# Expert units of a streaming-encoder kernel loaded as two halves of columns over two queues, with the gate stage and the kernel's beginning reordered

## The chip, the cores and the metric

The kernel runs on one core of one Trainium2 chip. The metric is the device time of one execution in microseconds (us), the median of several runs. All data is float32; the large products of the first half of the kernel are made in split form (a high and a low part of each operand).

## The reference, cut to what matters

One layer of an encoder block on 256 tokens of width 2048. After a normalized input projection, two attention groups and an output projection, the block ends with PEER, a retrieval over 128 x 128 single-neuron experts. The change lies in PEER and in the first microseconds of the input projection:

```python
h = rmsnorm(x, g_attn)
proj = h @ w_in                                   # the kernel's first stage
...
x = x + concat(y_a, y_b) @ w_o
hb = rmsnorm(x, g_ffn)
qr = (hb @ w_pq).reshape(b, t, 8, 2, 128)
sc = einsum('bthpd,hpnd->bthpn', qr, sub_keys)
s_top, i_top = top_k(sc, 16)                      # per half of the key
c_top, c_pos = top_k(s_top[..., 0, :, None] + s_top[..., 1, None, :], 16)
expert = i0 * 128 + i1
g = softmax(c_top)
a = gelu(einsum('bthkd,btd->bthk', u_tab[expert], hb))
x = x + einsum('bthk,bthkd->btd', g * a, v_tab[expert])
```

Each of the tables u_tab and v_tab has 16384 rows of 2048 floats, 134 MB.

## The kernel before, in words

The program is written per engine, with semaphores between the engines; the order on each engine is written out by hand.

**The first half** multiplies token tiles with pieces of w_in, w_o and w_pq. SyncE loads a piece of 512 KB (`load`, L355) into one of four buffers `raw`, ScalarE makes its high part (`split_hi`, L538), VectorE the low part (`split_lo`, L809), and TensorE makes twelve products per piece (`tall_unit`, L1307). At the very beginning the transposed tokens `xT` come in eight parts, each ahead of its piece of w_in on SyncE's queue; ScalarE and VectorE scale and split them (`norm_hi`, `norm_lo`). GpSimd's queue issues six small constants first (L437 to L442), then the rows of x and other weights, paced by `piece_used`, the count of half pieces that TensorE has finished.

**PEER** treats the 256 tokens in two ways. For 96 tokens (three of each four of the first 128, `N_SP`) the picked rows are fetched: GpSimd gathers one row of u_tab per partition and step, 1 MB in all, into one of five row buffers (`gather`, L471), and VectorE multiplies and sums it (`next_row`, L1128). A gather waits until the row five before it was used. There are 96 such rows of u_tab (`N_OWN`) and then 96 of v_tab; the latter are also paced by TensorE's count of finished units, from unit 117 to unit 250 (`PACE_FROM`, `PACE_TO`). For the other 160 tokens (`N_DN`) TensorE multiplies with the whole tables: 128 units of u_tab (`u_chunk`, L1511), then 128 of v_tab (`v_chunk`, L1567). A unit is 128 experts x 2048, 1 MB, 8 KB in each of 128 partitions, and is used in 16 products, each of two matmul instructions. Four ring buffers hold units; the transfer into a buffer is issued when the unit four before it is used up (`unit_used`): even units by SyncE (L404, L409), odd ones by ScalarE behind its gelu (`odd_unit`, L769). TensorE waits once per unit for its semaphore `unit_in`.

**The gates.** While TensorE works on the first 48 units of u_tab, VectorE finds the picks (`top_k`) and uses 28 rows. At unit 44 ScalarE takes the exponentials; VectorE then makes the gates' table of slots, uses rows in between, and from unit 48 (`FIRST_G`) on builds for each group of four tokens two one-hot tables (`hots`, L1179), which ScalarE scales by the gates (`hot_scale`, L755, eight and four operations, behind the gelu of a fixed unit, `scale_after`). TensorE multiplies them (`gate_group`, L1530), and VectorE applies them to finished activations (`gate`, L1190) and to each new unit's (`apply`, L1201). Gelu results of these units go through two buffers, so that ScalarE waits for the `apply` of two units before. TensorE does groups 0 and 1 behind units 50 and 51, and the others each behind an even unit; there are 40.

VectorE's program from unit 52 on is a loop in which rows stand between the gates' steps:

```python
for c in range(FIRST_G + 4, NKEY):
    ... hots(g + 1) if c is even, else gate(g)
    apply(c - 1)
    if rows_done[0] < N_OWN and c % 8 != 7:
        next_row()
    if c == WEIGH_AT: ...
```

Of the kernel before, what the change touches and what calls it, by code (L numbers as in the profile page):

```python
# [18 lines left out]
def build_block(nc, io):  # L19
# [5 lines left out]
    ACT = mybir.ActivationFunctionType  # L25
    AX = mybir.AxisListType.X
    ds = bass.ds
# [50 lines left out]
    with ExitStack() as ctx:  # L78
# [164 lines left out]
        unit_in = [sem(f"unit_in{i}") for i in range(NRING)]  # L243
# [4 lines left out]
        lent_in, acc_sum = sem("lent_in"), sem("acc_sum")  # L248
# [83 lines left out]
        WEIGH_AT = NKEY - 8  # L332
# [21 lines left out]
        def _(sp):  # L354
# [9 lines left out]
            for n in range(8):  # L364
                k = slice(2 * n, 2 * n + 2)
                sp.dma_start(xT[:, k, :], io["xT"][:, k, :]).then_inc(xT_in[n], 16)
                if n == 0:
                    sp.dma_start(gains[:, :], io["gains"]).then_inc(gain_in, 16)
                load(n, n, win[:, k, 0:512])
# [24 lines left out]

            for j in range(2):
                sp.wait_ge(lo_done, 2 * (B_U + 2 * j + 1) - 2 * (NRAW - 1))
                sp.dma_start(ring[j], u_unit(j)).then_inc(unit_in[j], 16)
            sp.wait_ge(piece_used, 2 * B_U)
            for j in range(2, NRING):
                sp.dma_start(ring[j], u_unit(j)).then_inc(unit_in[j], 16)  # L400
            with sp.Fori(1, NKEY // NRING) as i:
                for j in range(0, NRING, 2):
                    sp.wait_ge(unit_used, i * NRING + (j + 1 - NRING))
                    sp.dma_start(ring[j], u_unit(i * NRING + j)).then_inc(unit_in[j], 16)  # L404

            def v_units(i):
                for j in range(0, NRING, 2):
                    sp.wait_ge(unit_used, i * NRING + (NKEY + j + 1 - NRING))
                    sp.dma_start(ring[j], io["v_tab"][ds(i * (NRING * P) + j * P, P), :]).then_inc(unit_in[j], 16)  # L409
# [25 lines left out]
        def _(pool):  # L435

            pool.dma_start(acts[0:32, A_BIAS:A_BIAS + 512], io["bucket_hot"]).then_inc(hot_in, 16)  # L437
            pool.dma_start(acts[0:32, A_BIAS + 512:A_BIAS + 520], io["rel_bias"]).then_inc(hot_in, 16)
            pool.dma_start(iota[:, :], io["iota"]).then_inc(mask_in, 16)
# [88 lines left out]
        def _(act):  # L528
# [85 lines left out]

            act.wait_ge(gain_in, 16)
# [153 lines left out]
            def odd_unit(c):  # L769

                act.wait_ge(unit_used, c + 1 - NRING)
                src = io["u_tab"] if c < NKEY else io["v_tab"]
                act.dma_start(ring[c % NRING], src[c % NKEY * P:c % NKEY * P + P, :]).then_inc(unit_in[c % NRING], 16)

            for c in range(NKEY):
                gelu(c)
                if c % 2:
                    odd_unit(c + NRING)
                if c == FIRST_G - 4:
                    act.wait_ge(slot_ready, TT * NH)  # L780
                    nc.scalar.activation(slot[:, 2, :], slot[:, 2, :], ACT.Exp).then_inc(cexp_done, 1)
                if c in scale_after:
                    hot_scale(scale_after[c])
                if c == WEIGH_AT - 2:
                    act.wait_ge(row_used, N_OWN)
                    nc.scalar.activation(a_sel, a_sel, ACT.Gelu).then_inc(a_done, 1)
            for c in range(NKEY + 1, 2 * NKEY - NRING, 2):
                odd_unit(c + NRING)
# [9 lines left out]
        def _(dve):  # L798
# [35 lines left out]
            link(V.memset(kpad, 0.0))  # L834
# [383 lines left out]
            next_row(4)  # L1218
# [11 lines left out]
            next_row(2)  # L1230
            apply(FIRST_G)
            next_row()
# [8 lines left out]
            for c in range(FIRST_G + 4, NKEY):  # L1241
                if c % 2 == 0:
                    if g + 1 < N_GRP:
                        hots(g + 1)
                else:
                    gate(g)
                    g += 1
                apply(c - 1)
                if rows_done[0] < N_OWN and c % 8 != 7:
                    next_row()  # L1250
                if c == WEIGH_AT:
                    assert rows_done[0] == N_OWN
                    dve.wait_ge(a_done, 1)
                    dve.wait_ge(gsp_in, 48)
                    V.tensor_tensor(w_sp[:, 0:N_OWN], a_sel, w_sp[:, 0:N_OWN], ALU.mult).then_inc(w_ready, 1)
                    dve.wait_ge(acc_in, 16)
                    dve.wait_ge(mask_set, 2)
                    V.tensor_scalar(acc, acc, own_row, None, ALU.mult).then_inc(acc_set, 1)
                    dve.wait_ge(w_ready, 1)
                    dve.wait_ge(acc_set, 1)  # L1260
                if c > WEIGH_AT and c % 2:
                    next_row()
# [27 lines left out]
        def _(pe):  # L1290
# [99 lines left out]

            for j in range(8):
# [119 lines left out]
            def u_chunk(i, q):  # L1511
# [5 lines left out]
                pe.wait_ge(unit_in[q], i * 16 + 16)  # L1517
                for k in range(KD):
                    ins = mm(ps[:, q, 0:N_DN], ring[q][:, k * P:k * P + P], hF[:, k, :], start=k == 0, stop=k == KD - 1)  # L1519
# [47 lines left out]
            def v_chunk(i, q, first=False, last=False):  # L1567

                pe.wait_ge(unit_in[q], i * 16 + (16 * NKEY // NRING + 16))
                for k in range(KD):  # L1570
                    if first and k == 8:
                        pe.wait_ge(gelu_done, NKEY)
# [82 lines left out]
```

## Time and profile before

| | us |
|---|---|
| median of 3 runs | 1678.68 (1678.19 to 1679.05) |
| the profiled execution's own time | 1682.57 |
| its span, first to last instruction | 1680.8 |
| TensorE busy | 1653.3 |
| VectorE busy | 1019.2 |
| ScalarE busy | 503.3 |
| GpSimd busy | 293.3 |
| moved by DMA | 569.90 MB, 339 GB/s over the span |

Busy TensorE time is modelled for pipelined matmuls, so a short wait shows best as a gap named in a timeline. The span divides into: input and output projections and attention (to about 400 us), the query projection (to about 508), units of u_tab (514 to 1116, the gates from about 727 on) and units of v_tab (1116 to 1671).

### The profile page before, as it was taken

How to read it: one execution, taken by the hardware profiler on the slowest of the kernel's cores; microseconds unless marked ns; L12 is line 12 of the kernel's file. 1: busy time of each engine (PE TensorE's matmuls, PEld its weight loads, DVE VectorE, ACT ScalarE, POOL GpSimd, SP SyncE). 2: the span in 40 equal slices, each digit the busy share in tenths (PEclk: the TensorE clock that was granted, in tenths of full speed). 3: DMA queues.
4: the chain of work that ended last, by engine and by line, in shares of the span. 5: the costliest groups of instructions: out<-in, count | busy, mean ns of one | idle time of the engine just before them, and what ended most of it. 6: DMA issues, size and time to landing. Idle time of an engine off the chain costs nothing.

```text
span 1680.8 us, 28829 instructions
## 1 busy us (share of the span) xinstructions
PE 1653.3 (98%) x11428; PEld 1568.1 (93%) x11428; DVE 1019.2 (61%) x1708; ACT 503.3 (30%) x1346; POOL 293.3 (17%) x252
## 2 busy tenths in 40 slices
PE   7999999999999999989999999999999999999999
PEld 5768888888999999979999999999999999999998
DVE  5426695767778999767777667663334333433343
ACT  6547567656551000134454444420000000000000
POOL 1020000000003222322212111122212212223220
PEclk9999999999999999999999999999999999999999
DMA  9764445466648999999999999999999999999996
GB/s 337 240 142 131 138 132 194 138 223 204 224 154 347 421 403 421 397 400 421 394 422 406 421 408 422 375 388 416 417 415 417 417 416 422 422 422 422 421 417 236
DMA packets 107056, 569.90 MB, mean 339 GB/s; under 512 B 11280, under 2 KB 13456, under 8 KB 48208
## 3 DMA queue, kind: packets, MB, share of 16 engines
q1 hardware_dynamic: 57056, 216.51, 34.8%
q0 software_dynamic: 31792, 220.50, 32.7%
q10 hardware_dynamic: 18144, 132.13, 19.2%
q8 instruction: 29, 0.48, 0.1%
q14 instruction: 35, 0.29, 0.0%
HBM read 563.04 MB, written 4.46 MB: 338 GB/s over the span
## 4 chain that ended last, share of the span: by engine, by line
PE 78%; DVE 12%; DMA 6%; ACT 1%; issue 1%; POOL 1%; SPq 0%; DVEq 0%; ACTq 0%; POOLq 0%
PE ps L1574 32%; PE ps L1519 19%; PE ps L1315 5%; PE ps L1317 5%; PE ps L1316 5%; DVE late L1136 3%; PE ps L1334 2%; PE ps L1468 2%; PE ps L1536 2%; PE ps L1470 2%; PE ps L1469 2%; DMA raw<-in_w_in 1%; DMA acts<-in_u_rows,sel 1%; DMA late<-in_u_rows,sel 1%; DVE w_lo L817 1%
## 5 line engine op out<-in xcount | busy, mean ns | idle before, releaser
L1140 DVE SCALAR_TENSOR_TENSOR acts<-late,sel,acts 128x2048 f32<-128x2048 f32 x77 | 181.1, 2351 | 246.5 <-DMA late<-in_v_tab,sel 246.1
L1519 PE MATMUL ps<-acts,raw 128*128 128x160 f32 x2048 | 289.3, 301 | 0.0
L1519 PE MATMUL ps<-acts,late 128*128 128x160 f32 x2048 | 287.9, 300 | 0.0
L1574 PE MATMUL ps<-acts,late 128*128 (+1 forms) x2048 | 284.2, 299 | 0.0
L1574 PE MATMUL ps<-acts,raw 128*128 (+1 forms) x2048 | 283.6, 300 | 0.2 <-DMA raw<-in_v_tab 0.2
L1519 PEld LDWEIGHTS ps<-acts,raw 128*128 128x128 f32 x2048 | 282.1, 191 | 0.0
L1519 PEld LDWEIGHTS ps<-acts,late 128*128 128x128 f32 x2048 | 280.5, 190 | 0.0
L1574 PEld LDWEIGHTS ps<-acts,raw 128*128 128x128 f32 x2048 | 279.9, 190 | 0.6 <-issue 0.6
L1574 PEld LDWEIGHTS ps<-acts,late 128*128 128x128 f32 x2048 | 280.1, 190 | 0.1
L817 DVE TENSOR_TENSOR w_lo<-raw,w_hi 128x512 fp32r<-128x512 f32 (+1 forms) x288 | 188.8, 682 | 134.9 <-ACT w_hi L544 132.9
L1315 PE MATMUL ps<-w_hi,hT_hi 128*128 128x512 f32 (+1 forms) x448 | 185.7, 415 | 13.5 <-DVE w_lo L817 13.2
L544 ACT ACTIVATE w_hi<-raw 128x512 fp32r<-128x512 f32 (+1 forms) x288 | 170.2, 622 | 90.2 <-PE ps L1470 42.3
L1136 DVE SCALAR_TENSOR_TENSOR late<-late,acts 128x2048 f32<-128x2048 f32 x76 | 173.1, 2287 | 14.3 <-DMA late<-in_u_rows,sel 14.1
L1317 PE MATMUL ps<-w_hi,hT_lo 128*128 128x512 f32 (+1 forms) x448 | 174.4, 389 | 0.0
L1316 PE MATMUL ps<-w_lo,hT_hi 128*128 128x512 f32 (+1 forms) x448 | 173.8, 388 | 0.0
L483 POOL DMA_INDIRECT late<-in_v_tab,sel x77 | 106.9, 1389 | 370.7 <-PE ps L1574 261.5
L793 ACT ACTIVATE acts<-ps 128x320 f32<-128x320 f32 x8 | 3.5, 437 | 555.9 <-PE ps L1574 555.7
L483 POOL DMA_INDIRECT late<-in_u_rows,sel x76 | 95.8, 1261 | 302.8 <-DVE late L1136 236.6
L1315 PEld LDWEIGHTS ps<-w_hi,hT_hi 128*128 128x128 f32 x448 | 84.7, 189 | 36.3 <-issue 14.8
L1316 PEld LDWEIGHTS ps<-w_lo,hT_hi 128*128 128x128 f32 x448 | 84.8, 189 | 17.5 <-issue 3.1
L1317 PEld LDWEIGHTS ps<-w_hi,hT_lo 128*128 128x128 f32 x448 | 84.4, 188 | 17.2
L1198 DVE TENSOR_TENSOR acts<-acts,ps 128x512 f32<-128x512 f32 x40 | 46.6, 1166 | 84.6 <-PE ps L1536 84.6
(220 smaller groups left out, 1575.7 us busy)
## 6 DMA issues: line engine op xcount, KB each, us to landing
raw<-in_w_in SPq DMA_DIRECT2D x72, 512.0 KB, 3.7
raw<-in_u_tab SPq DMA_DIRECT2D x33, 1024.0 KB, 9.7
late<-in_u_tab SPq DMA_DIRECT2D x33, 1024.0 KB, 9.9
raw<-in_v_tab SPq DMA_DIRECT2D x32, 1024.0 KB, 9.3
raw<-in_v_tab ACTq DMA_DIRECT2D x32, 1024.0 KB, 9.2
late<-in_v_tab SPq DMA_DIRECT2D x32, 1024.0 KB, 9.1
late<-in_v_tab ACTq DMA_DIRECT2D x32, 1024.0 KB, 9.3
raw<-in_u_tab ACTq DMA_DIRECT2D x31, 1024.0 KB, 9.7
```

The lines of the kernel that those rows point to most:

```text
L483: pool.indirect_dma_start(row[n % NROW], None, table, bass.IndirectOffsetOnAxis(ap=idx[:, k:k + 1], axis=0)).then_inc(row_in[n % NROW], 16)
L544: nc.scalar.activation(whi[(2 * j + half) % NPART][:, 0:w], raw[j % NRAW][:, half * w:half * w + w], ACT.Copy).then_inc(hi_done, 1)
L817: V.tensor_tensor(wlo[slot_no][:, 0:w], raw[j % NRAW][:, half * w:half * w + w], whi[slot_no][:, 0:w].bitcast(F32), ALU.subtract).then_inc ...
L1136: V.scalar_tensor_tensor(row[n % NROW], row[n % NROW], 1.0, hs[turn % 2], ALU.mult, ALU.mult, accum_out=a_sel[:, n:n + 1]).then_inc(row_us ...
L1140: V.scalar_tensor_tensor(acc, row[n % NROW], w_sp[:, n - N_OWN:n - N_OWN + 1], acc, ALU.mult, ALU.add).then_inc(row_used, 1)
L1198: V.tensor_tensor(a, a, ps[:, 4 + g % 2, :].rearrange("p (t e) -> p t e", t=4), ALU.mult).then_inc(gated, 1)
L1315: mm(out, hT_hi[:, k, t], whi[part][:, 0:w], start=start and kk == 0, stop=False)
L1316: mm(out, hT_hi[:, k, t], wlo[part][:, 0:w], start=False, stop=False)
L1317: ins = mm(out, hT_lo[:, k, t], whi[part][:, 0:w], start=False, stop=stop and kk == 1)
L1334: ins = mm(ps[:, bank, :], src[:, k, b * P:b * P + P], w[:, k, :], start=k == 0, stop=k == ks - 1)
L1519: ins = mm(ps[:, q, 0:N_DN], ring[q][:, k * P:k * P + P], hF[:, k, :], start=k == 0, stop=k == KD - 1)
L1574: ins = mm(ps[:, pair_bank(k // 2), at:at + N_DN], ring[q][:, k * P:k * P + P], acts[:, ds(i * (4 * N_DN) + q * N_DN, N_DN)], start=first ...
```

## The change

1. A unit is loaded in two halves of 1024 columns (4 KB in each partition): SyncE issues the first half of every unit, ScalarE the second half of every unit from the fifth on (`second_half`); both halves of the first four units are issued by SyncE. Each half has its own semaphore, and TensorE waits for the second one ahead of the ninth of its 16 products.
2. Behind the slots' table VectorE uses 2 rows rather than 4, none behind the first hot tables (2 before), and none between the first two `apply` (1 before). In the loop it leaves out a row at every sixteenth unit rather than at every eighth, and the weighing step of the gathered rows stands at unit 122 rather than 120.
3. At the beginning `xT`'s first part and `gains` are issued by ScalarE, so w_in's first piece is SyncE's first transfer; four of the six constants on GpSimd's queue wait until TensorE has finished a half piece; ScalarE runs a one-element operation, with the load of its function table, ahead of its first wait for data; TensorE makes five products of zeros ahead of its first wait.

```diff
-        unit_in = [sem(f"unit_in{i}") for i in range(NRING)]
+        unit_in = [sem(f"unit_in{i}") for i in range(2 * NRING)]
...
-        WEIGH_AT = NKEY - 8
+        WEIGH_AT = NKEY - 6
...
             for n in range(8):
                 k = slice(2 * n, 2 * n + 2)
-                sp.dma_start(xT[:, k, :], io["xT"][:, k, :]).then_inc(xT_in[n], 16)
-                if n == 0:
-                    sp.dma_start(gains[:, :], io["gains"]).then_inc(gain_in, 16)
+                if n:
+                    sp.dma_start(xT[:, k, :], io["xT"][:, k, :]).then_inc(xT_in[n], 16)
                 load(n, n, win[:, k, 0:512])
...
             with sp.Fori(1, NKEY // NRING) as i:
-                for j in range(0, NRING, 2):
+                for j in range(NRING):
                     sp.wait_ge(unit_used, i * NRING + (j + 1 - NRING))
-                    sp.dma_start(ring[j], u_unit(i * NRING + j)).then_inc(unit_in[j], 16)
+                    sp.dma_start(ring[j][:, 0:HALF], u_unit(i * NRING + j)[:, 0:HALF]).then_inc(unit_in[2 * j], 16)
...
+            pool.wait_ge(piece_used, 1)
             pool.dma_start(iota[:, :], io["iota"]).then_inc(mask_in, 16)
...
+            act.dma_start(xT[:, 0:2, :], io["xT"][:, 0:2, :]).then_inc(xT_in[0], 16)
+            act.dma_start(gains[:, :], io["gains"]).then_inc(gain_in, 16)
+            act.wait_ge(warm_set, 1)
+            nc.scalar.activation(table_warm, carrier, ACT.Copy)
...
-            def odd_unit(c):
+            def second_half(c):
 
                 act.wait_ge(unit_used, c + 1 - NRING)
                 src = io["u_tab"] if c < NKEY else io["v_tab"]
-                act.dma_start(ring[c % NRING], src[c % NKEY * P:c % NKEY * P + P, :]).then_inc(unit_in[c % NRING], 16)
+                act.dma_start(ring[c % NRING][:, D // 2:D], src[c % NKEY * P:c % NKEY * P + P, D // 2:D]).then_inc(unit_in[2 * (c % NRING) + 1], 16)
 
             for c in range(NKEY):
                 gelu(c)
-                if c % 2:
-                    odd_unit(c + NRING)
+                second_half(c + NRING)
...
-            link(V.memset(kpad, 0.0))
+            V.memset(carrier, 0.0).then_inc(warm_set, 1)
+            V.memset(kpad, 0.0).then_inc(warm_set, 1)
...
-            next_row(4)
+            next_row(2)
...
             hots(0)
             hots(1)
-            next_row(2)
             apply(FIRST_G)
-            next_row()
             apply(FIRST_G + 1)
             next_row()
             gate(0)
...
-                if rows_done[0] < N_OWN and c % 8 != 7:
+                if rows_done[0] < N_OWN and c % 16 != 15:
                     next_row()
...
+            pe.wait_ge(warm_set, 2)
+            for _ in range(5):
+                mm(ps[:, 6, 0:256], kpad[:, 0, :], early[:, 1024:1280], start=True, stop=True)
...
-                pe.wait_ge(unit_in[q], i * 16 + 16)
                 for k in range(KD):
+                    if k % 8 == 0:
+                        pe.wait_ge(unit_in[2 * q + k // 8], i * 16 + 16)
                     ins = mm(ps[:, q, 0:N_DN], ring[q][:, k * P:k * P + P], hF[:, k, :], start=k == 0, stop=k == KD - 1)
```

**VectorE, from the hot tables of groups 0 and 1 on, before.** L1184 builds one-hot tables, L1136 uses a gathered row, L1208 is `apply`, L1198 is `gate`.

```order
L1184 TENSOR_TENSOR early<-iota,slotT 128x512 x2
L1184 TENSOR_TENSOR acts<-iota,slotT 128x512 x2
L1136 SCALAR_TENSOR_TENSOR late,sel<-late,acts 128x2048 x2
L1208 TENSOR_TENSOR acts<-acts,early 128x160
L1136 SCALAR_TENSOR_TENSOR late,sel<-late,acts 128x2048
L1208 TENSOR_TENSOR acts<-acts,early 128x160
L1136 SCALAR_TENSOR_TENSOR acts,sel<-acts 128x2048
L1198 TENSOR_TENSOR acts<-acts,ps 128x4x128
L1184 TENSOR_TENSOR early<-iota,slotT 128x512 x2
```

The same place now; the lines have moved on by seven.

```order
L1191 TENSOR_TENSOR early<-iota,slotT 128x512 x2
L1191 TENSOR_TENSOR acts<-iota,slotT 128x512 x2
L1215 TENSOR_TENSOR acts<-acts,early 128x160 x2
L1143 SCALAR_TENSOR_TENSOR acts,sel<-acts 128x2048
L1205 TENSOR_TENSOR acts<-acts,ps 128x4x128
L1191 TENSOR_TENSOR early<-iota,slotT 128x512 x2
```

Between the tables of group 1 and those of group 2 stood four rows; one is left, behind both `apply`.

**ScalarE, at the first units of u_tab, before.** L753 is the gelu of a unit, L773 the issue of an odd unit's transfer.

```order
L753 ACTIVATE acts<-ps 128x160 [waits x2_stored]
L753 ACTIVATE acts<-ps 128x160 [waits unit_used]
L773 DMA raw<-in_u_tab 128x2048 [waits unit_used]
L753 ACTIVATE acts<-ps 128x160 [waits unit_used] x2
L773 DMA late<-in_u_tab 128x2048 [waits unit_used]
```

The same place now:

```order
L760 ACTIVATE acts<-ps 128x160 [waits x2_stored]
L780 DMA raw<-in_u_tab 128x1024 [waits unit_used]
L760 ACTIVATE acts<-ps 128x160 [waits unit_used]
L780 DMA raw<-in_u_tab 128x1024 [waits unit_used]
L760 ACTIVATE acts<-ps 128x160 [waits unit_used]
L780 DMA late<-in_u_tab 128x1024 [waits unit_used]
```

There is an issue of half the size behind every gelu, where there was one of the full size behind every second; SyncE's loop likewise has one of half the size per unit.

## Rows read from the trace of the kernel before

**Rows 1.** Busy time by stage: PE, PEld, DVE, ACT, POOL, clock, DMA share, GB/s

```profile
530.00:600.00 70.00, 70.00 (x517) 69.97 (x516) 63.38 (x196) 4.86 (x16) 18.43 (x11) 1.00 1.01 422
...
850.00:1055.00 205.00, 204.83 (x1645) 201.88 (x1645) 146.98 (x183) 95.20 (x308) 39.12 (x39) 1.00 1.01 416
...
1400.00:1600.00 200.00, 200.00 (x1474) 200.00 (x1473) 82.47 (x36) 0.00 (x0) 49.84 (x35) 1.00 1.01 422
```

**Rows 2.** The chain that ended last, in v_tab's stage: start, us, what

```profile
1364.06 13.10 DMA raw<-in_v_tab
1377.29 293.12 PE ps L1574 x2156
```

**Rows 3.** Timeline of PE at the wait for that unit

```profile
1377.29 8.01 PE L1574 MATMUL ps<-acts,raw 128*128 x57 [0.22 <-DMA raw<-in_v_tab]
```

**Rows 4.** DMA issues of the page: KB each, median us to landing

```profile
late<-in_u_tab SPq DMA_DIRECT2D x33, 1024.0 KB, 9.9
```

**Rows 5.** Timeline of PE where the gates begin

```profile
746.09 0.84 PE L1536 MATMUL ps<-acts 128*128 128x128 bf16 x12 [2.88 <-ACT acts L766]
...
757.18 1.46 PE L1536 MATMUL ps<-early 128*128 128x128 bf16 x12 [5.85 <-ACT early L766]
```

**Rows 6.** Busy time in the stretch of that second wait, columns as in rows 1

```profile
754.00:762.00 8.00, 4.82 (x26) 4.82 (x27) 7.90 (x11) 3.28 (x12) 4.12 (x6) 0.57 1.01 422
```

**Rows 7.** Timeline of DVE where the gates begin

```profile
728.97 1.29 DVE L1184 TENSOR_TENSOR acts<-iota,slotT 128x512 bf16<-128x512 f32 x2
...
734.18 2.29 DVE L1136 SCALAR_TENSOR_TENSOR late<-late,acts 128x2048 f32<-128x2048 f32 x1 [3.92 <-DMA late<-in_u_rows,sel]
...
741.67 0.32 DVE L1208 TENSOR_TENSOR acts<-acts,early 128x160 f32<-128x160 f32 x1
...
748.77 2.29 DVE L1136 SCALAR_TENSOR_TENSOR acts<-acts 128x2048 f32<-128x2048 f32 x1 [1.20 <-DMA acts<-in_u_rows,sel]
...
750.99 1.16 DVE L1198 TENSOR_TENSOR acts<-acts,ps 128x512 f32<-128x512 f32 x1
...
752.06 1.28 DVE L1184 TENSOR_TENSOR early<-iota,slotT 128x512 bf16<-128x512 f32 x2
```

**Rows 8.** Timeline of ACT where the gates begin

```profile
733.76 0.30 ACT L753 ACTIVATE early<-ps 128x160 f32<-128x160 f32 x1 [4.04 <-PE ps L1519]
...
742.09 0.30 ACT L753 ACTIVATE early<-ps 128x160 f32<-128x160 f32 x1 [4.18 <-DVE acts L1208]
...
753.38 2.44 ACT L762 ACTIVATE early<-early,acts 128x128 bf16<-128x128 bf16 x8 [5.41 <-DVE early L1184]
755.85 1.28 ACT L766 ACTIVATE early<-early,slotT 128x128 bf16<-128x128 bf16 x4
...
774.15 0.30 ACT L753 ACTIVATE early<-ps 128x160 f32<-128x160 f32 x1 [4.83 <-PE ps L1519]
```

**Rows 9.** Timeline of ACT in the steady gate stage, gelu of two odd units

```profile
1058.94 0.30 ACT L753 ACTIVATE early<-ps 128x160 f32<-128x160 f32 x1 [4.83 <-PE ps L1519]
...
1068.42 0.30 ACT L753 ACTIVATE early<-ps 128x160 f32<-128x160 f32 x1 [4.83 <-PE ps L1519]
```

**Rows 10.** Timeline of POOL: gathers of rows 32 and 37

```profile
722.14 2.40 POOL L483 DMA_INDIRECT late<-in_u_rows,sel  x1 [16.70 <-DMA sel<-sel]
...
736.75 0.94 POOL L483 DMA_INDIRECT late<-in_u_rows,sel  x1 [6.88 <-DVE late L1136]
```

**Rows 11.** SyncE's DMA queue, 1400 to 1600 us: packets, MB, share of 16 engines

```profile
q1 hardware_dynamic: 3327, 24.12, 29.0%
```

**Rows 12.** The same queue with pieces of w_pq, 422 to 426 us

```profile
q1 hardware_dynamic: 389, 1.40, 85.7%
```

**Rows 13.** The same queue with pieces of w_pq, 412 to 500 us

```profile
q1 hardware_dynamic: 4043, 14.70, 50.4%
```

**Rows 14.** ACT's first table load, and DMA in the chain's beginning

```profile
3.57 1.28 ACT L564 ACT_TABLE_LOAD   x1 [3.57 <-DMA acts<-in_xT]
...
17.73 12.63 DMA raw<-in_w_in
```

More of the change, by code:

```diff
@@ L247, in build_block @@
         hs_in, idx_in, gsp_in, mask_set, acc_set, turn_kept = sem("hs_in"), sem("idx_in"), sem("gsp_in"), sem("mask_set"), sem("acc_set"), sem("turn_kept")
-        lent_in, acc_sum = sem("lent_in"), sem("acc_sum")
+        lent_in, acc_sum, warm_set = sem("lent_in"), sem("acc_sum"), sem("warm_set")
         gsp_ready, a_done, w_ready, acc_in = sem("gsp_ready"), sem("a_done"), sem("w_ready"), sem("acc_in")
@@ L393, in u_unit @@
                 return io["u_tab"][ds(v * P, P), :]
+            HALF = D // 2
             for j in range(2):
                 sp.wait_ge(lo_done, 2 * (B_U + 2 * j + 1) - 2 * (NRAW - 1))
-                sp.dma_start(ring[j], u_unit(j)).then_inc(unit_in[j], 16)
+                for h in range(2):
+                    sp.dma_start(ring[j][:, HALF * h:HALF * h + HALF], u_unit(j)[:, HALF * h:HALF * h + HALF]).then_inc(unit_in[2 * j + h], 16)
             sp.wait_ge(piece_used, 2 * B_U)
             for j in range(2, NRING):
-                sp.dma_start(ring[j], u_unit(j)).then_inc(unit_in[j], 16)
+                for h in range(2):
+                    sp.dma_start(ring[j][:, HALF * h:HALF * h + HALF], u_unit(j)[:, HALF * h:HALF * h + HALF]).then_inc(unit_in[2 * j + h], 16)
             with sp.Fori(1, NKEY // NRING) as i:
-                for j in range(0, NRING, 2):
+                for j in range(NRING):
                     sp.wait_ge(unit_used, i * NRING + (j + 1 - NRING))
-                    sp.dma_start(ring[j], u_unit(i * NRING + j)).then_inc(unit_in[j], 16)
+                    sp.dma_start(ring[j][:, 0:HALF], u_unit(i * NRING + j)[:, 0:HALF]).then_inc(unit_in[2 * j], 16)
             def v_units(i):
-                for j in range(0, NRING, 2):
+                for j in range(NRING):
                     sp.wait_ge(unit_used, i * NRING + (NKEY + j + 1 - NRING))
-                    sp.dma_start(ring[j], io["v_tab"][ds(i * (NRING * P) + j * P, P), :]).then_inc(unit_in[j], 16)
+                    sp.dma_start(ring[j][:, 0:HALF], io["v_tab"][ds(i * (NRING * P) + j * P, P), 0:HALF]).then_inc(unit_in[2 * j], 16)
             with sp.Fori(0, 8) as i:
@@ L786, in _ @@
                     nc.scalar.activation(a_sel, a_sel, ACT.Gelu).then_inc(a_done, 1)
-            for c in range(NKEY + 1, 2 * NKEY - NRING, 2):
-                odd_unit(c + NRING)
+            for c in range(NKEY, 2 * NKEY - NRING):
+                second_half(c + NRING)
             for p in range(KD // 2):
@@ L1567, in v_chunk @@
             def v_chunk(i, q, first=False, last=False):
-                pe.wait_ge(unit_in[q], i * 16 + (16 * NKEY // NRING + 16))
                 for k in range(KD):
+                    if k % 8 == 0:
+                        pe.wait_ge(unit_in[2 * q + k // 8], i * 16 + (16 * NKEY // NRING + 16))
                     if first and k == 8:
```

## The prediction, made before the changed kernel ran

> **What bounds the kernel now.** I read the stage table first. From 530 us on TensorE is busy for the whole of each stretch, and the 16 DMA engines are too, at 416 to 422 GB/s [rows 1]. VectorE and ScalarE have room: 147 and 95 of 205 us in the gate stage. So two limits lie on top of each other, and a step counts only as far as it moves the one that ends last.
>
> TensorE's own pace is 293.12 us for 2156 matmuls, 0.136 us each, so 4.35 us for a unit of 32 [rows 2]. A gate group adds the rest of a pair: two gelus of odd units lie 9.48 us apart [rows 9], which less two units leaves 0.78 us.
>
> The transfers' pace: 1.049 MB at 422 GB/s is 2.485 us for a unit or a gathered row. In the gate stage 7 rows go with 8 units, so a unit's share is 2.485 x 1.875 = 4.66 us, against 9.48/2 = 4.74 us of TensorE. In v_tab's stage 96 rows are paced over 133 units, 0.722 each: 4.28 against 4.35 us. Both leave only some 1.7%. A unit's transfer may take three units of TensorE, 13.05 us; the median takes 9.9 [rows 4], and one of v_tab took 13.10 [rows 2] and made TensorE wait 0.22 us [rows 3].
>
> TensorE's one large loss is where the gates begin: it waits 2.88 and 5.85 us for ScalarE's scaled tables [rows 5]. In the stretch of the second wait the granted clock is 0.57 on average, so partly the 1.2 GHz level, and the group behind it takes 1.46 us instead of 0.84 [rows 5, 6]. All in all: between the gelus of units 49 and 55 lie 774.15 - 733.76 = 40.39 us [rows 8], and the work is 6 x 4.35 + 4 x 0.78 = 29.2. **11.2 us are lost.**
>
> **Part 1, the rows taken out of the gates' beginning.** VectorE finishes the tables of groups 0 and 1 at 730.26, and then stands in front of rows still in transfer, four waits from 3.92 to 1.20 us [rows 7]. So the first `apply` comes at 741.67 although its gelu was done, ScalarE's gelu of unit 50 waits for it until 742.09, and the table of group 2 is begun at 752.06, for which ScalarE waits 5.41 us [rows 7, 8]. In the new order both `apply` follow the tables at once (unit 49's at 734.1, behind its gelu), and the single row left, number 30, was gathered long before: 2.3 us, to 736.7. I step on with the same durations. ScalarE scales group 0 from 734.2 for 2.45 + 1.28 us, to 737.9; TensorE ends unit 50 at 738.1 and does the group, to 738.9; VectorE gates it to 740.1 (1.16) and builds group 2's table to 741.4 (1.28). ScalarE scales group 1 from 738.9 to 742.7, ahead of unit 51's end at 743.2, and group 2 from 743.7 to 747.5, ahead of unit 52's end at 748.3. No wait is left, and with it goes the low clock. **-11.2 us**; the bound from the other side is that the larger wait stays.
>
> Rows held back: gathers 35 and 36 start only when rows 30 and 31 are used (about 737 and 744), where before five were issued from 722.14 on [rows 10]. They are wanted at about 760 and 765, so nothing waits for them. Five rows must be made up in the loop: 64 rows from unit 52 on at 15 in 16 units end at unit 119, as the 59 before did, ahead of the weighing at 122. VectorE gains one row of 2.29 us per 16 units, 0.14 us a unit, covered by its idle quarter [rows 1]. The price is in the transfers: 0.0625 x 2.485 = 0.155 us a unit.
>
> **Part 2, the halves.** The additional issues lie beside free time of SyncE and behind ScalarE's gelu, where an issue stood already behind every second one. TensorE's additional wait, when already met, costs nothing: 2156 matmuls with 67 met waits keep one pitch of 0.136 us [rows 2]. Bytes stay equal, but packets are 4 KB rather than 8. SyncE's queue moved 24.12 MB in 29.0% of 3200 engine-us, 26.0 GB/s per engine [rows 11]. With w_pq's packets of 4 KB and little beside it, 1.40 MB took 85.7% of 64, 25.5 GB/s [rows 12], 2% less. The far end is all of w_pq's stage, 14.70 MB in 50.4% of 1408, 20.7 GB/s [rows 13], a quarter less, but there the engines mostly idled between pieces; the near end is nothing. I take 2%, so 2.535 us a unit.
>
> With both, a unit of the gate stage asks for 2.535 + 0.9375 x 2.485 = 4.865 us of transfer against 4.74 of TensorE. Over the 68 units from 52 to 119 the arrears are 8.5 us. They are first paid from the time that a transfer may take. Both halves of a unit now run side by side, behind the previous unit's only; sharing the engines with a row, a unit needs about 2 x 2.535 us and some 2 us to be reported (an estimate, from the 9.9 us of a unit that shared with two others [rows 4]), so 7 to 8 us of 13.05. That pays about 6; **+2.4 us** wait remains (0 to 8.5). In v_tab's stage the demand is 2.535 + 1.794 = 4.33 against 4.35, with x2's reload of 1.3 MB on top, which before was enough for the 13.10: **+1.0** (0 to 4). At u_tab's beginning, where five rows and four units are in flight at once at 422 GB/s [rows 1], I put **+1.0** (0 to 2).
>
> The Trainium skill ("DMA: Bandwidth & Descriptors", section Bandwidth) speaks against the halves: it asks for transfers of at least 1 MiB for 75% of peak. By that rule the 512 KB halves would lose far more than 2%; the traced queue at 85.7% with 512 KB pieces doesn't bear it out.
>
> **Part 3, the beginning.** ScalarE's table load of 1.28 us [rows 14] goes beside the wait for data, w_in's first piece is issued two issues sooner, and four constants leave its way. But up to about 30 us transfers end last: the piece issued at 17.73 takes 12.63 us [rows 14], and the bytes until then are the same, since the constants only move behind the first half piece. TensorE's five products at the start warm a stretch that waits for data anyway. I take **-1.0** (0 to -2.5).
>
> **The sum**: -11.2 - 1.0 + 2.4 + 1.0 + 1.0 = -7.8 us. Against the profiled execution's 1682.57 that is 1674.8. The median of the runs lies 3.9 us lower, at 1678.68, and I put the same difference there: **1670.9 us**.
>
> **The rivals.**
> - *Transfers cover themselves.* Without the three added waits: -12.2, **1666.5**. For it: units waited only 0.22 us at 98% load [rows 3], and waiting by halves gives the second half 2.2 us more. Chance 0.20.
> - *The wait moves.* Rows 34 to 36 come later than I step them, or one scaled table is late, and a wait of the size of the larger one (5.85) stays with its low clock: -7.8 + 5.9 = -1.9, **1676.8**. ScalarE supports it: in the steady stage it ends a table just as its group is due. Chance 0.15.
> - *The transfers bound the gate stage: slower.* If a half costs 3.5% more, a unit takes 2.57 us; two queues of 4 KB packets against one of 8 KB rows hold only half of the engines, which is less than the units' share, so units are late rather than rows, and nothing is paid from the slack. Then each unit asks 4.90 against 4.74, 68 x 0.16 = 11; v_tab's 4.366 against 4.35, 2; the reload 3; the beginning of u_tab 1.5. -12.2 + 17.5 = +5.3, **1684.0**. It turns slower once less than about a third of the arrears can be paid from slack. Against it: 422 GB/s held for 200 us with all queues active [rows 1]. Chance 0.13.
> - *Halves flow like all of w_pq's stage*, 26% longer, 3.12 us: 0.71 x 68 + 0.56 x 128 + 0.2 x 48 = 130 us more, about **1797**. The skill's rule points this way. Chance 0.02.
>
> **How the numbers follow.** My forecast has 0.50. Its own range is 1668 to 1675. With the first rival at the low end, and the second and a part of the third at the high one: 1665.5 to 1681. A measurement tells 0.2%, 3.4 us. Faster by more: the forecast, the first rival and a third of the second, 0.74; within: the rest of the second and mild forms of the third, 0.13; slower 0.13.
>
> **What would show it.** Right: VectorE's tables of group 2 are built near 741, TensorE's waits of 2.88 and 5.85 are gone and the clock there is 1.00; TensorE shows a few waits named for transfers of u_tab between units 90 and 120, 2 to 3 us together; the share of DMA stays at 1.0 through the gate stage at 410 to 420 GB/s; halves land in 7 to 10 us. Wrong: DMA waits above 8 us in the gate stage, GB/s below 405 at full share, a wait over 3 us near 745 to 760, or a beginning that differs by more than 2.5 us at 60 us.

## The result, and the profile after

The changed kernel takes **1690.41 us** (median of 4 runs, 1688.94 to 1691.05), the kernel before 1678.87 (4 runs, 1678.19 to 1680.11): a ratio of 1.0063, 95% interval 1.0051 to 1.0075. That is **slower** by 11.5 us, where 7.8 us less were forecast, and it lies above the range (to 1681.0). The profiled execution of the changed kernel took 1690.0 us, with a span of 1688.2.

Its busy time by stage, with the columns of [rows 1]:

```profile
530.00:600.00 70.00, 64.90 (x453) 63.11 (x452) 66.69 (x200) 4.25 (x14) 18.95 (x11) 0.98 1.02 411
534.00:574.00 40.00, 37.68 (x256) 36.35 (x256) 38.48 (x118) 2.34 (x8) 9.99 (x6) 0.96 1.02 414
...
850.00:1055.00 205.00, 203.40 (x1631) 200.12 (x1629) 147.37 (x182) 91.13 (x295) 42.16 (x40) 1.00 1.02 415
1400.00:1500.00 100.00, 99.56 (x732) 99.21 (x732) 40.87 (x19) 0.00 (x0) 15.88 (x16) 1.00 1.02 414
```

The engines' share of DMA is full as before, but they move 411 to 415 GB/s rather than 416 to 422, and TensorE is no longer always busy. What it waited for (us in total, times, longest), from the changed kernel's list of waits for the whole execution:

```profile
...
PE ps L1584 <- DMA raw<-in_v_tab: 5.2, 7, 2.5
PE ps L1528 <- DMA raw<-in_u_tab: 3.8, 4, 2.6
PE ps L1584 <- DMA late<-in_v_tab: 2.1, 5, 0.5
...
PE ps L1545 <- ACT early L773: 0.9, 2, 0.5
PE ps L1545 <- ACT acts L773: 0.5, 1, 0.5
PE ps L1528 <- DMA late<-in_u_tab: 0.5, 2, 0.3
...
```

The two waits of [rows 5], 8.7 us for ScalarE's scaled tables, have shrunk to 1.4 us. In their place stand 11.6 us of waits for units of u_tab and v_tab, where before there were 0.22 [rows 3]. The timeline of TensorE at u_tab's beginning:

```profile
533.75 10.63 PE L1528 MATMUL ps<-acts,raw 128*128 128x160 f32 x64 [2.60 <-DMA raw<-in_u_tab]
544.22 4.51 PE L1528 MATMUL ps<-acts,late 128*128 128x160 f32 x32
548.98 4.58 PE L1528 MATMUL ps<-acts,late 128*128 128x160 f32 x32 [0.26 <-DMA late<-in_u_tab]
553.94 4.61 PE L1528 MATMUL ps<-acts,raw 128*128 128x160 f32 x32 [0.37 <-DMA raw<-in_u_tab]
559.04 4.58 PE L1528 MATMUL ps<-acts,raw 128*128 128x160 f32 x32 [0.49 <-DMA raw<-in_u_tab]
```

The first 64 matmuls behind the wait of 2.60 take 10.63 us rather than 8.86, and the granted clock over 534 to 574 us is 0.96: the wait costs more than its length. Later units begin 4.96, 5.10 us and so on apart, rather than 4.35. The shown gaps are only 0.3 to 0.5 us because the matmuls before them are drawn longer, so I count by the starts of units.

The table below gives the start of a unit's first product on TensorE, minus the start of the same unit in the trace of before. "Halves alone" and "order alone" are two experiments told of below (`e2_halves_only` and `e8_order_only`).

| unit | before, us | changed | halves alone | order alone |
|---|---|---|---|---|
| 0 (u_tab) | 515.51 | -2.45 | -2.12 | -0.95 |
| 16 | 585.12 | +6.79 | +6.89 | -1.00 |
| 48 | 724.87 | +6.79 | +6.89 | -1.01 |
| 54 (gates begun) | 764.47 | -4.49 | -4.38 | -12.28 |
| 80 | 887.76 | -4.49 | -4.40 | -12.30 |
| 128 (v_tab) | 1115.91 | -2.10 | -3.40 | -12.55 |
| 160 | 1255.00 | +0.68 | -3.40 | -12.55 |
| 200 | 1429.55 | +7.38 | +2.67 | -11.42 |
| 255 | 1668.61 | +7.38 | +2.82 | -11.42 |

The changed kernel loses 9.2 us over units 0 to 16, gains 11.3 where the gates begin, loses 2.4 in the gate stage and 9.5 in v_tab's. The gain is the forecast one; the losses are not. The first row also shows by how much one execution differs from another: "halves alone" and "order alone" have the old beginning and still start 2.1 and 1.0 us sooner. The trace of before is itself of an execution of 1682.57 us, 3.7 above its kernel's median, and that of the changed kernel of one of 1690.0. So the table ends at +7.4, while the medians lie 11.5 apart: it shows where time goes, and not the size of the whole to a microsecond or two.

Where the gates begin, TensorE's timeline now has no wait, and the granted clock of 748 to 756 us is 1.00, against 0.57 over 754 to 762 us in [rows 6]:

```profile
744.75 0.84 PE L1545 MATMUL ps<-early 128*128 128x128 bf16 x12
745.43 4.57 PE L1528 MATMUL ps<-acts,late 128*128 128x160 f32 x32
749.83 0.83 PE L1545 MATMUL ps<-acts 128*128 128x128 bf16 x12
750.50 4.57 PE L1528 MATMUL ps<-acts,raw 128*128 128x160 f32 x32
754.91 0.83 PE L1545 MATMUL ps<-early 128*128 128x128 bf16 x12
```

What each DMA queue moved between 548 and 558 us (packets, MB, share of 16 engines; q0 carries GpSimd's rows, q1 SyncE's transfers, q10 ScalarE's), in the kernel before:

```profile
q0 software_dynamic: 251, 1.81, 43.5%
q10 hardware_dynamic: 182, 1.36, 32.7%
q1 hardware_dynamic: 144, 1.05, 25.2%
```

The same window of the changed kernel:

```profile
q0 software_dynamic: 283, 2.06, 50.0%
q1 hardware_dynamic: 283, 1.03, 25.7%
q10 hardware_dynamic: 284, 1.03, 25.5%
```

Three queues with work, 283, 283 and 284 packets. But a packet of a row is 8 KB and one of a half is 4 KB, so the rows get half of all bytes, and both halves together the other half. A unit then lands only as often as a row does: 2.10 MB for both at 414 GB/s are 5.07 us, which is TensorE's new pace. The chain that ended last shows how long the halves that TensorE waited for were in flight (start, us, what), where a whole unit's median was 9.9 [rows 4]:

```profile
517.75 15.96 DMA raw<-in_u_tab
...
540.22 13.68 DMA raw<-in_u_tab
...
558.74 15.35 DMA raw<-in_u_tab
...
1131.63 15.15 DMA late<-in_v_tab
...
1260.22 15.34 DMA raw<-in_v_tab
```

That is more than the 13.05 us that a transfer may take.

### The profile page after: what moved, and what is told of

Its sections match the earlier page's. It is cut to its first block, busy times and chain, and to the rows that moved or that the text cites. A ratio compares the mean times of both kernels' runs of the same rounds, so it can differ in the third digit from the quotient of the medians.

```text
span 1688.2 us, 29406 instructions
## 1 busy us (share of the span) xinstructions
PE 1661.3 (98%) x11438; PEld 1571.4 (93%) x11438; DVE 1019.6 (60%) x1709; ACT 503.5 (30%) x1347; POOL 272.5 (16%) x252
## 4 chain that ended last, share of the span: by engine, by line
PE 82%; DMA 12%; DVE 2%; ACT 2%; issue 1%; POOL 0%; ACTq 0%; SPq 0%; DVEq 0%
PE ps L1584 28%; PE ps L1528 26%; PE ps L1320 5%; PE ps L1322 5%; PE ps L1321 5%; DMA raw<-in_v_tab 3%; DMA raw<-in_u_tab 3%; DMA late<-in_v_tab 3%; PE ps L1339 2%; PE ps L1476 2%; PE ps L1478 2%; PE ps L1477 2%; PE ps L1545 1%; DMA sel<-sel 1%; DMA late<-in_u_rows,sel 1%
## 5 line engine op out<-in xcount | busy, mean ns | idle before, releaser
L486 POOL DMA_INDIRECT late<-in_v_tab,sel x77 | 89.1, 1157 | 386.4 <-PE ps L1584 230.8
L760 ACT ACTIVATE early<-ps 128x160 f32<-128x160 f32 x80 | 24.3, 303 | 201.8 <-PE ps L1528 177.4
```

Of the source, the lines that this page charges most:

```text
L486: pool.indirect_dma_start(row[n % NROW], None, table, bass.IndirectOffsetOnAxis(ap=idx[:, k:k + 1], axis=0)).then_inc(row_in[n % NROW], 16)
```

## The experiments

The theories. **A, turns:** the engines take packets from the queues with work in turn; halving a unit's packets halves the weight of its queue against the rows. **B, price of small packets:** bytes in 4 KB packets flow more slowly. **C, order:** the new order of rows makes a backlog that the units run into. **D, the join:** a unit needs two transfers over two queues, and the later one sets it. Where a median is given for before, it is that of runs on the same chip beside the experiment. Most of the expected totals were missed by some microseconds; the stages say more than they.

### Order and beginning without the halves; halves without them

`e1_order_start` is the changed kernel with whole units, as before:

```diff
-                for j in range(NRING):
+                for j in range(0, NRING, 2):
                     sp.wait_ge(unit_used, i * NRING + (j + 1 - NRING))
-                    sp.dma_start(ring[j][:, 0:HALF], u_unit(i * NRING + j)[:, 0:HALF]).then_inc(unit_in[2 * j], 16)
+                    sp.dma_start(ring[j], u_unit(i * NRING + j)).then_inc(unit_in[j], 16)
```

> The changed kernel with whole units again (one transfer of 1 MB and 8 KB packets per unit, even units by SyncE, odd ones by ScalarE); the new order of the gates and the new beginning stay. Theory A (the halves lose: the DMA engines take packets from their queues in turn, so two queues of 4 KB packets hold as much as one queue of 8 KB row packets, and a unit lands every 5.05 us while rows are in backlog): the 2.45 us of the beginning and the 11.3 us of the gates' beginning are gained, the waits for units at the start of u_tab (9.2 us) and in v_tab (9.5 us) are gone; 1665 to 1667 us. Theory B (4 KB packets only move fewer bytes, 414 against 422 GB/s): the same, 1665 to 1668. Theory C (the new order of the rows makes the backlog): waits for units stay in v_tab or move into the gate stage, 1673 or more.

Measured: 1671.15 us against 1680.07, ratio 0.9943 (0.9927 to 0.9960). TensorE waits for no unit of u_tab, so the halves are what makes them late. The total lies above the 1665 to 1668 of theories A and B and below C's 1673: in the gate stage 4.2 us are lost between units 91 and 114, where scaled tables are late.

`e2_halves_only` is the kernel before with the halves, and nothing else of the change.

> The kernel before with nothing but the halves of columns over two queues. Theories A and B: the waits for units of 9.2 us at the start of u_tab and of about 9.5 us in v_tab come, the gates' first wait of 11.2 us stays; 1695 to 1700 us. Theory C (order): the halves alone cost at most the 2% of packet size, under 4 us; 1679 to 1683.

Measured: 1686.61 against 1680.07, ratio 1.0044 (1.0028 to 1.0061). The halves alone make it slower, with the old order: C is not needed. The 1695 to 1700 us of theories A and B were missed all the same, and the table above shows why. This kernel has the old order of rows, and yet it gains 11.3 us between units 48 and 54, as much as the reordered ones. TensorE's timeline there:

```profile
744.86 0.84 PE L1539 MATMUL ps<-early 128*128 128x128 bf16 x12
745.54 4.57 PE L1522 MATMUL ps<-acts,late 128*128 128x160 f32 x32
749.94 0.83 PE L1539 MATMUL ps<-acts 128*128 128x128 bf16 x12
750.61 4.57 PE L1522 MATMUL ps<-acts,raw 128*128 128x160 f32 x32
755.01 0.83 PE L1539 MATMUL ps<-early 128*128 128x128 bf16 x12
```

VectorE's timeline tells why. The tables of group 1, and the first row behind them, which in [rows 7] came at 734.18 after a wait of 3.92 us:

```profile
735.76 1.29 DVE L1186 TENSOR_TENSOR acts<-iota,slotT 128x512 bf16<-128x512 f32 x2
736.97 2.28 DVE L1138 SCALAR_TENSOR_TENSOR late<-late,acts 128x2048 f32<-128x2048 f32 x1
```

The tables are 6.8 us later than in [rows 7], because TensorE, and with it the slots' transposition, is 6.9 us later. The gather of the row behind them did not move back with it. In GpSimd's timeline it is issued at 713.90, where it was 722.14 [rows 10]:

```profile
713.90 0.96 POOL L486 DMA_INDIRECT late<-in_u_rows,sel  x1 [13.04 <-DMA sel<-sel]
```

So between this row's gather and the end of the tables lie 23.1 us, where it was 8.1, and it has landed. The four behind it were issued by 731.77 (728.57 before) and are used from 739.17 on. The time lost on units at u_tab's beginning was given back here, if not by itself alone: how much the sooner gather does and how much the later tables was not tried apart.

### Where one part of the change is undone or done alone

`e8_order_only` is the kernel before with part 2's order of rows, `e9_start_only` the kernel before with the new beginning.

> The kernel before with nothing but the new order of rows and gates. The gates' beginning gains 11.2 us, the gate stage gives about 4.3 back, no start gain: 1672 to 1675 us. If the gain of the beginning (2.5 to 3.6 us in the traces) is real and independent, this run lies that much above the run with whole units, new order and new beginning.

Measured: 1670.97 against 1679.5, ratio 0.9947 (0.9928 to 0.9966), -8.5 us. That is under the 1672 to 1675 expected. Its gain lies between units 48 and 54 (-11.3 by the table); it loses nothing in the gate stage and 1.1 us in v_tab's. There is no wait for units of u_tab.

> The kernel before with nothing but the new beginning (ScalarE issues xT's first part and gains, four constants later, table load and five products ahead of the data). In the traces unit 0 of u_tab starts 2.5 to 3.6 us sooner with the new beginning, but in two runs with the old one it started 1.0 and 2.1 us sooner too. Theory G (a gain of its own of 1 to 2 us, the rest is difference between executions): 1677.0 to 1678.5 beside about 1679.5. Forecast as on record: -1.0. Theory H (full 2.5 to 3.6): 1676 or less.

Measured: 1678.77 against 1679.16, ratio 0.9995 (0.9987 to 1.0004): no gain that can be told. The old order's wait stands here, but once, with 6.45 us. Between units 48 and 54 this trace (of an execution of 1678.69 us) loses 2.1 us less than that of before (1682.57), so the old order costs 9.2 us there in one execution and 11.3 in the other.

Alone, the parts come to -8.5 (order), +6.5 (halves) and -0.4 (beginning), -2.4 in all; together they are +11.5. Of the 14 us between, 9.2 to 11.3 are the same gain counted twice: halves or order, either removes the wait. The rest is of the size of what differs from unit 80 on: 11.9 us are lost in the changed kernel, 7.2 with the halves alone. Of these 4.7 us, 2.8 come over units 128 to 136, at v_tab's beginning, where the changed kernel waits for four units and the other for none.

### How the halves are cut, and the queues

`e3_part_halves` cuts a unit by partitions, 0 to 63 and 64 to 127, so that packets stay at 8 KB; TensorE waits for both ahead of its first product:

```diff
-                    sp.dma_start(ring[j][:, 0:HALF], u_unit(i * NRING + j)[:, 0:HALF]).then_inc(unit_in[2 * j], 16)
+                    sp.dma_start(ring[j][0:64, :], io["u_tab"][ds(i * (NRING * P) + j * P, 64), :]).then_inc(unit_in[2 * j], 16)
```

> The changed kernel with halves of partitions instead of columns: each half 64 partitions of 8 KB, first half by SyncE, second by ScalarE, both awaited ahead of the unit's first product. Packets are 8 KB again. Theory A (packets in turn): the units' two queues hold two thirds of the engines in a backlog, no wait for units; 1665 to 1668. Theory B (bytes per packet): also 1665 to 1668, 422 GB/s. Theory D (two queues, the join of two transfers or the issue of a half behind ScalarE's gelu makes units late, whatever the packets): waits stay, 1686 or more.

Measured: 2298.93 against 1680.07, ratio 1.371 (1.3654 to 1.3766), a miss of every theory. Its busy time by stage:

```profile
530.00:600.00 70.00, 50.90 (x346) 48.72 (x347) 40.98 (x121) 3.04 (x10) 5.62 (x6) 0.95 1.02 261
...
850.00:1055.00 205.00, 142.12 (x1019) 138.30 (x1019) 90.47 (x111) 60.31 (x195) 26.66 (x28) 0.85 1.00 254
```

The engines are busy all the time and move 254 to 261 GB/s; the rows, which are unchanged, slow down with the units (0.94 MB between 548 and 558 us, where the changed kernel moved 2.06). So this run says nothing on A or D, and the same packets had to be cut in another way.

`e5_even_odd` takes even partitions by SyncE and odd ones by ScalarE:

```diff
-                    sp.dma_start(ring[j][:, 0:HALF], u_unit(i * NRING + j)[:, 0:HALF]).then_inc(unit_in[2 * j], 16)
+                    sp.dma_start(ring[j][0:P:2, :], by_two("u_tab")[0, ds(i * (NRING * 64) + j * 64, 64), :]).then_inc(unit_in[2 * j], 16)
```

> The changed kernel with halves of alternate partitions: SyncE loads the 64 even ones, ScalarE the 64 odd ones, 8 KB packets, both awaited ahead of the first product. It asks the question of the run with partitions 0 to 63 and 64 to 127 again, without filling one half of the partitions at a time. Theory A (packets in turn): units hold two thirds of the engines in a backlog, the waits for units at the start of u_tab (9.2 us in the changed kernel) and in v_tab (9.5) go, 1668 to 1673 us as with whole units. Theory D (two queues or the join make units late): the waits stay, 1686 or more. Theory E (any transfer to 64 partitions is slow): far slower, over 1750.

Measured: 1675.23 (10 runs) against 1679.5, ratio 0.9973 (0.9964 to 0.9983). Halves, two queues, a wait for both, the new order: all is there, and it is faster than before. Only the packet has its 8 KB again. Its queues between 548 and 558 us:

```profile
q0 software_dynamic: 237, 1.74, 41.9%
q10 hardware_dynamic: 186, 1.25, 30.1%
q1 hardware_dynamic: 185, 1.24, 29.8%
```

The units have about 60% of the bytes. The time lies 2 us above A's range and 11 below D's. Each measured against its own runs of before, it is 4 to 5 us slower than whole units (`e1_order_start`). By its unit starts it loses 1.1 us over units 0 to 16, where `e1_order_start` loses nothing, and 5.0 us in the gate stage (units 54 to 128), where that one loses 4.2. This bounds what D can be.

`e4_one_queue` is the changed kernel with both column halves issued by SyncE.

> The changed kernel with both halves of columns issued by SyncE, one behind the other, and none by ScalarE: packets of 4 KB, in one queue. Theory A: in a backlog one 4 KB packet of a unit goes with each 8 KB packet of rows, so a unit lands only every 2.57 + 2 x 2.49 = 7.5 us while rows are in backlog; TensorE waits over 3 us per unit there, more than 20 us on top of the changed kernel: 1710 us or more, and the row queue moves about 1.8 to 2 times the bytes of the unit queue in the first 50 us of u_tab. Theory B: as the changed kernel, 1688 to 1692. Theory D: faster than the changed kernel, since no half is issued behind the gelu.

Measured: 1697.0 (one run) against 1680.07. The units have one turn in two rather than two in three. Between 528 and 538 us:

```profile
q0 software_dynamic: 381, 2.74, 66.0%
q1 hardware_dynamic: 381, 1.43, 35.4%
```

Equal packets again, and twice the bytes for the rows. But theory A's total, 1710 us or more, was missed by 13 us: by the starts of units this kernel loses 9.5 us over units 0 to 16, hardly more than the changed kernel's 9.2, and 11.2 in the gate stage rather than 2.4. Between 548 and 558 us q1 already has 56.2%. That the backlog of at most five rows is used up by then fits this, but wasn't tried apart.

`e6_rows_4k` is the changed kernel with each row gathered in two transfers of 4 KB packets, so that all packets are equal:

```diff
-                pool.indirect_dma_start(row[n % NROW], None, table, bass.IndirectOffsetOnAxis(ap=idx[:, k:k + 1], axis=0)).then_inc(row_in[n % NROW], 16)
+                for h in range(2):
+                    pool.indirect_dma_start(row[n % NROW][:, D // 2 * h:D // 2 * h + D // 2], None, table, bass.IndirectOffsetOnAxis(ap=idx[:, k:k + 1], axis=0), element_offset=D // 2 * h).then_inc(row_in[n % NROW], 16)
```

> The changed kernel with each gathered row fetched as two gathers of 1024 columns, so that all three queues have 4 KB packets. Theory A: in the first 50 us of u_tab the three queues move equal packets and so a third of the bytes each, units two thirds; TensorE's waits for units there fall from 9.2 us to under 2, and rows come later (VectorE waits more). Theory B (fewer bytes per packet of 4 KB): waits for units grow, since now all packets are small. Total 1680 to 1695, rows then being what is late in the gate stage.

Measured: 1701.62 (one run) against 1679.5, above the 1680 to 1695 expected. Between 548 and 558 us the rows' queue moved 1.63 MB, the others 1.25 and 1.22. TensorE waits for no unit at all in the whole execution; its waits are these:

```profile
PE ps L1546 <- ACT early L774: 10.1, 3, 7.0
PE ps L1546 <- ACT acts L774: 9.1, 2, 8.0
PE ps L1321 <- DVE w_lo L824: 6.0, 7, 2.8
```

It reaches unit 54 at -14.41 by the table's count, as the order forecasts, and then the rows are late, VectorE's tables behind them, and TensorE waits through ScalarE. Another 10.2 us are lost behind unit 254, where the last rows of v_tab come late too (VectorE uses the last one from 1684.14 us on). So smaller packets for the rows only move the wait. This is the sharpest test of A: still smaller packets, and the waits for units vanish. It also sizes B, by its busy time by stage:

```profile
530.00:600.00 70.00, 70.00 (x517) 70.00 (x517) 62.54 (x197) 5.17 (x17) 30.05 (x22) 1.00 1.03 409
...
1400.00:1600.00 200.00, 200.00 (x1475) 200.00 (x1474) 76.75 (x35) 0.00 (x0) 62.05 (x65) 1.00 1.03 410
```

With every packet of rows and units at 4 KB the engines move 409 and 410 GB/s in these two stretches, with a mix 411 and 414, with 8 KB 422.

`e11_three_rows` is the changed kernel with at most three rows in flight for the first 20 rows rather than five.

```diff
-                if n >= NROW:
-                    pool.wait_ge(row_used, n + 1 - NROW)
+                if n >= NROW or n >= 3:
+                    pool.wait_ge(row_used, n + 1 - (3 if n < 20 else NROW))
```

> The changed kernel with at most three gathers in flight instead of five for rows 0 to 19, the start of u_tab. Theory A (units wait only while rows stand in backlog beside them, since packets go in turn): a shorter backlog, so the waits there fall from 9.2 us to under 5. Theory B (fewer bytes per packet): bytes and packets are equal, 8 to 10 us stay. The rest as in the changed kernel; 1683 to 1688 with A.

Measured: 1690.87 (one run) against 1679.16, above the 1683 to 1688 of theory A. By the starts, unit 16 stands at +1.68 after -2.94 for unit 0: 4.6 us lost there rather than 9.2, as a shorter backlog should make it. Another 4.2 us are lost over units 32 to 48, where five may be in flight again; so that unit 54 stands at -5.44, against -4.49. In v_tab's stage it loses some 11 us, the changed kernel 9.5, and nothing is left of the gain at the end.

### Versions that beat both

`e7_rows_spread` is `e1_order_start` with two rows used ahead of the wait for the exponentials, a row left out at every ninth unit, and the weighing step at unit 124:

```diff
+            next_row(2)
             dve.wait_ge(cexp_done, 1)
...
-                if rows_done[0] < N_OWN and c % 16 != 15:
+                if rows_done[0] < N_OWN and c % 9 != 8:
```

> Whole units, the new beginning, the new gates' order, but rows asked for more evenly: two rows are used ahead of the wait for the exponentials (where VectorE idles 9.4 us), and 62 rows rather than 64 are spread over 70 units rather than 68 (weighing at unit 124). Theory F (in the run with whole units the 4.3 us lost between units 80 and 112 come from the rows' demand of 15 in 16 units, 4.82 us of transfer per 4.74 us unit): those 4.3 us fall below 1.5, 1666 to 1669 us. If they came from something else in the new order: 1670 to 1673.

Measured: 1669.41 against 1679.5 (1666 to 1669 were expected), ratio 0.9938 (0.9919 to 0.9957). Units 54 to 128 keep their lead (-13.81 to -14.39), where `e1_order_start` fell from -14.90 to -10.67.

`e10_reload_spread` is that kernel with SyncE's eight transfers of x2's reload spread over 16 groups of units rather than eight, since 1.4 us were lost there.

> The run with whole units, new beginning, new gates' order and rows spread over 70 units, and x2's reload of 1.3 MB in addition spread over 64 units of v_tab rather than 32. The 1.4 us that TensorE lost there between units 160 and 192 come from the reload on top of 98% load: they go, 1.4 us less than that run's 1669.4, so 1667.5 to 1668.5. If it is only the paced rows that made the unit late: no difference.

Measured: **1668.16** (5 runs, 1667.63 to 1669.49) against 1679.16, ratio 0.9932 (0.9919 to 0.9945), the fastest of all. By its starts v_tab's stage loses 0.4 us rather than 1.4. That it beats the one before it by 1.2 us is at the edge of what can be told across chips.

## Why the prediction was wrong, step by step

**The limits** were read rightly: TensorE and the DMA engines on top of each other with 1.7% between them. The conclusion was drawn only for the sum of bytes, not for who gets them.

**Part 1, -11.2.** Right in size by the trace that it was read from: 11.3 us, no wait, clock 1.00 (by the runs, the order alone gained 8.5 us, between 5.7 and 12.1). VectorE builds group 2's tables at 746.85 rather than 741, but everything there is 6.8 us late. Wrong as a term of the sum. The wait of [rows 5] hangs on the rows' lead over VectorE's tables, and with the halves that lead is larger: they alone remove the wait. The changed kernel's reordering therefore bought nothing over the halves alone. I had weighed this part against the trace of before, and not against the kernel with the other part in it.

**Part 2, the step that failed:** the waits of +1.0 at u_tab's beginning (0 to 2) and +1.0 in v_tab's stage (0 to 4). They measured 9.2 and 9.5. I had reckoned that the halves of a unit share the engines with a row, and so land in 7 to 8 us. With a standing backlog of rows the halves that TensorE waited for took 13.2 to 16.0 us, since half of all bytes went to the rows as long as there were any. The slack of three units doesn't help against a share for long: a unit lands 0.7 us later than TensorE is done with one (5.07 less 4.35), and when the slack is used up, TensorE runs at the transfers' pace. u_tab's beginning has such a backlog by design (five rows at once, more as VectorE uses them), and rows are in flight at v_tab's beginning too. In v_tab's stage turns are not shown as clearly: in the changed kernel between 1275 and 1295 us, with x2's reload on SyncE's queue, the three queues moved 444, 738 and 631 packets. What is shown there is the effect of the packets' size: with 8 KB for all (`e5_even_odd`) the stage loses 0.6 us, with 4 KB for all (`e6_rows_4k`) nothing.

**The price of small packets** was put at 2%. In the mixed stretches 422 GB/s became 411 to 414, and with 4 KB packets alone 409 to 410, some 3%. That is within the bounds given, and it isn't what made the units late: `e6_rows_4k` pays the most and has no wait for a unit.

**The gate stage, +2.4.** The table gives 2.4, but that is luck. I expected late units between 90 and 120; no unit was late there, rows were. VectorE waits some 1.3 us for most rows from 940 us on, where the kernel before waits for none, and once long:

```profile
993.74 1.18 DVE L1205 TENSOR_TENSOR acts<-acts,ps 128x512 f32<-128x512 f32 x1
995.02 0.32 DVE L1215 TENSOR_TENSOR acts<-acts,early 128x160 f32<-128x160 f32 x1
1003.24 2.29 DVE L1143 SCALAR_TENSOR_TENSOR acts<-acts 128x2048 f32<-128x2048 f32 x1 [7.90 <-DMA acts<-in_u_rows,sel]
```

With whole units the same order lost 4.2 us in `e1_order_start` and nothing in `e8_order_only`, whose unit 128 starts 0.3 us further ahead than its unit 54. So 15 rows in 16 units can leave too little room, and why they did so in one kernel and not in the other is not shown. Spreading the rows (`e7_rows_spread`) ended it.

**Part 3, -1.0.** Measured alone, -0.4, and not to be told from nothing. The table load does come at 1.69 us, beside the wait, but the first product stands at 8.20 us against 8.00, since ScalarE now waits for `gains`. The products of zeros end at 5.4 us, and over 8 to 11 us the granted clock is 0.53, about its lower level: the real products take 0.63 us each until 11.3 us (until 10.7 before), and 0.39 to 0.40 behind that.

**The rivals.** The third named the right mechanism, two queues of 4 KB packets against one of 8 KB rows, at a chance of 0.13. I placed it in the gate stage, where rows are short of supply rather than in excess, and priced it as 1684.0; it acts wherever rows pile up. Its argument against, that 422 GB/s were held with all queues active, was no argument: the total held here too, within 3%. The first rival fell with the waits for units. The second didn't come, since no wait stands near 745 to 760 us, and the fourth fell with the 409 to 414 GB/s. The signs that I had named for being wrong looked mostly at the gate stage. TensorE waited for no unit there; the losses lay in front of it and behind it. The rule of the Trainium skill ("DMA: Bandwidth & Descriptors", section Bandwidth), 1 MiB transfers, is not borne out: 512 KB halves kept 98% of the rate. The same page of the Trainium skill (section Queues, rings and completion order) states that a DMA engine goes round the queues that have work and takes a packet from each. The windows agree, at 283, 283 and 284 packets; this rule was the one to weigh.

What stays open: what remains of D (at most the 4 to 5 us by which `e5_even_odd` lies above whole units), how much of the loss in v_tab's stage comes from turns and how much from x2's reload beside them, and why transfers by 64 neighbouring partitions are so slow, which no run here shows.

## What to carry to other kernels

Where queues compete, count packets and not bytes: in these windows a queue's share was its packet size against that of the others with work, and making a critical transfer's packets smaller hands its share to whoever is behind it. Before two gains are added, ask whether the first one removes the wait that the second one is about; here the halves alone and the reordering alone each removed the same 11.3 us of the traces. Read a change's stages by the starts of units, since the end hides what one stage gave back to another.

## What the runs showed of the hardware that was not expected

- Turns by packet: 283, 283 and 284 packets of three queues in 10 us with 2.06, 1.03 and 1.03 MB; with two queues 381 and 381.
- Transfers of 64 neighbouring partitions, over two queues, moved 254 to 268 GB/s at a full share of the engines, and slowed the rows with them; alternate partitions, with packets of the same size, 410 to 422.
- Packets of 4 KB against 8 KB in a full stretch (1400 to 1600 us): 410 against 422 GB/s.
